# One split operation per engine over 2048 columns in place of two over 1024, in the first stage of a two-layer decoder trunk

## The chip, the cores and the metric

One core of one Trainium2 chip runs the whole kernel. The metric is the device time of one execution in microseconds (us), the median of the runs shown. One further execution was taken by the hardware profiler; durations below come from it. PE is TensorE, ACT ScalarE, DVE VectorE, POOL GpSimd, SP the SyncE queue that issues most loads.

## What is computed

Two layers act on 512 tokens of width 1024, in float32. Layer 0 is, cut to what matters here:

```python
proj = xn @ w_in          # 512x1024 @ 1024x7168: the stage of this change
a_b, a_c, a_x, a_gate, b_u, b_v, b_gate = split(proj)
y_a = a_b * conv3(a_c * a_x) * silu(a_gate)
v   = layernorm(b_v)
y_b = b_u * (tril(w_s) @ v + b_s) * silu(b_gate)
y   = concat(y_a, y_b) @ w_out
h   = h + rmsnorm(y); h = h + sigmoid(rmsnorm(h) @ w_g) * (p @ w_p)
```

Layer 1 is an mLSTM mixer with the same tail. The change touches the product `xn @ w_in` of layer 0 alone.

## The kernel before

**Split operands.** A float32 product is made of three products in the form fp32r: high by high, high by low, low by high. So each weight block in `raw7` is split: ACT copies it to `w7_hi` (line L647, in `hi7`), which rounds it, and DVE subtracts that from the block and writes `w7_lo` (L1077, in `lo7`). A block is 128 partitions by 2048 columns. Both helpers do it in two halves of 1024 columns, with one semaphore step for each half.

**Units and steps.** The 7168 output columns of layer 0 are worked in seven units (0 to 6). The product of a unit is a 2x2 block product of Strassen's kind with seven small products, p1 to p7, in place of eight. From unit 1 on their order is `ORDER = (1, 5, 6, 3, 2, 7, 4)`, here steps k0 to k6. So k2 is p6, k3 is p3, k5 is p7 and k6 is p4. On PE a small product (`product(u, p, tp)`) is two tiles tp of 12 matmuls of 512 columns (L1721, L1723, L1724). The operands of p5, p6, p7 and p4 are sums of blocks: p6's is made on DVE (`s6_add`, L1084), the others by transfers that add into `raw7`, which POOL issues (`add_in`, L525). POOL issues the one for p7 when the split of p3 is done (`late_sums`).

**Queues.** Each engine works its queue in the order written. On ACT and DVE the iteration k of unit u holds the split for the step two ahead (`hi7(7u + k + 2)`, `lo7(7u + k + 2)`). There are three buffers for split blocks (`RING = 3`), so the split for a step waits until the product three steps back has ended (`prod_done`). The split for k6 (p4) is thus in iteration k4, that for the next unit's k0 (p1) in iteration k5, that for k5 (p7) in iteration k3.

Around the splits stand the combinations of the small products. Those that matter below:

- `c_make(u, 0)` (DVE, L1155) is in iteration k2 behind `lo7`. PE's step k3 (p3) waits for it (`c_made`). In units 2 to 5 `conv` (L1202, L1205) and `c_make(u, 1)` follow it.
- `s5_make(u, 0)` (DVE; L1165, in unit 0 L1162) is in iteration k5 behind `lo7` and `z_make` (L1187) or `wide_silu` (L1209). PE's step k6 (p4) waits for it (`s5_made`).
- In units 2 to 5 iteration k4 on DVE is `lo7`, `g_make` twice, `conv`. On ACT, iterations k2 and k4 have `conv_copy` (L743, L744) ahead of `hi7`, and those copies wait for PE's `conv_transposes` (L1737, L1744) in front of steps k2 and k4.
- In unit 6 PE has `mix_transposes` (L1766) and `mix` (L1755) between steps. `mix_transposes(0)` in front of k3 waits for `mix_make(0)` (DVE, L1225), which is in DVE's iteration k2 behind `lo7` and `c_make`; `mix_transposes(1)` in front of k4 waits for `mix_make(1)`, behind `lo7` in iteration k3. On ACT, `b_copy` (L694) in iteration k1 waits for `wide_silu` of iteration k0 on DVE, behind that iteration's `lo7`; `y_high` (L759) and `s5_copy` follow.

PE's wait for the split is in `product`: half by half, on `w7_lo_ready`.

Of the kernel before, what the change touches and what calls it, by code (L numbers as in the profile page):

```python
# [25 lines left out]
F32 = mybir.dt.float32  # L26
F32R = mybir.dt.float32r
ACT = mybir.ActivationFunctionType
ALU = mybir.AluOpType
# [19 lines left out]
RING = 3  # L49
# [4 lines left out]
STEPS = [(u, p) for u in range(UNITS) for p in (ORDER if u else ORDER_FIRST)]  # L54
# [11 lines left out]
def x_buffer(u):  # L66
    return BV if u % 2 else BX


def source(u, p):  # L70

    if p in (1, 6, 4):
        return x_buffer(u)
    if p == 7 and u == 0:
        return BV
    return {5: BA, 3: BY, 7: BY, 2: BZ}[p]
# [89 lines left out]
def trunk(nc, x, p_in, slots, g_rows, ln_rows, w_mix, b_mix, conv_w, gate_bias, head_g, out):  # L166
# [3 lines left out]
    def region(at, *spec):  # L170

        made = []
        for name, shape, dtype in spec:
            size = 4
            for n in shape[1:]:
                size *= n
            made.append(nc.alloc_sbuf_tensor_at(name, shape, dtype, offset=at))
            at += (size + 31) // 32 * 32
        assert at <= nc.sbuf_usable_end, at
        return made  # L180
# [24 lines left out]
    w7_hi, w7_lo = region(W_AT, ("w7_hi", [P, RING, SLOT], F32R), ("w7_lo", [P, RING, SLOT], F32R))  # L205
    raw7, = region(R_AT, ("raw7", [P, 5, SLOT], F32))
# [125 lines left out]
    s6_sum = sem("s6_sum")  # L332
    added_in = {5: sem("s5_added_in"), 7: sem("s7_added_in"), 4: sem("s4_added_in")}
    a_in = sem("a_raw_in")
    w7_hi_ready = sem("w7_hi_ready")
    w7_lo_ready = sem("w7_lo_ready")
# [253 lines left out]
    def _(act):  # L590
# [35 lines left out]
        def hi7(g):  # L626

            u, p = STEPS[g]
            if p == 1:
                act.wait_ge(x_raw_in, 16 * (u + 1))  # L630
            if p == 2:
                act.wait_ge(z_raw_in, 16 * (u + 1))
            if p == 3:
                act.wait_ge(y_raw_in, 16 * (u + 1))
            if p == 5 and u:
                act.wait_ge(added_in[5], 16 * u)
            if p in (7, 4):
                act.wait_ge(added_in[p], 16 * (u + 1))
            if g >= RING:
                act.wait_ge(prod_done, 2 * (g - RING) + 2)  # L640
            for half in range(2):
                c = slice(half * SLOT // 2, (half + 1) * SLOT // 2)
                if p == 5 and u == 0:
                    act.wait_ge(s5_sum, half + 1)
                if p == 6:
                    act.wait_ge(s6_sum, 2 * u + half + 1)
                act.activation(w7_hi[:, g % RING, c], raw7[:, source(u, p), c], ACT.Copy).then_inc(w7_hi_ready, 1)  # L647
# [27 lines left out]
        left(0, 0, 1, 11)  # L675
        left(0, 1, 2, 12)
        hi7(0)
        x_squares(2)
        left(1, 0, 1, 11)
        left(1, 1, 2, 12)  # L680
        x_squares(3)
        left(2, 0, None, 21)
        left(2, 1, 4, None)
        hi7(1)
        left(3, 0, None, 21)
        left(3, 1, 4, None)
# [75 lines left out]
        for k in range(7):  # L762
            if k == 0:
                b_copy(0, 0)
                left_sum(5, f5)
                b_copy(0, 1)
            if k == 1:
                left_sum(6, f11)
            if k == 2:
                left_sum(3, f12)  # L770
                left_sum(7, f21)
                for tp in range(2):
                    v_copy0(a_of, 2, 0, tp, tp, a_free)
            if k == 3:
                for tp in range(2):
                    s5_copy(0, tp)
            if k == 5:
                for tp in range(2):
                    v_copy0(c_of, 3, 4, tp, tp, c_free)
            hi7(k + 2)  # L780
# [244 lines left out]
    def _(dve):  # L1025
# [44 lines left out]
        def lo7(g):  # L1070

            if g >= RING:
                dve.wait_ge(prod_done, 2 * (g - RING) + 2)
            for half in range(2):
                c = slice(half * SLOT // 2, (half + 1) * SLOT // 2)
                dve.wait_ge(w7_hi_ready, 2 * g + half + 1)
                dve.tensor_tensor(w7_lo[:, g % RING, c], raw7[:, source(*STEPS[g]), c],  # L1077
                                  w7_hi[:, g % RING, c].bitcast(F32), ALU.subtract).then_inc(w7_lo_ready, 1)
# [59 lines left out]
        left(0, 0, 1)  # L1138
        left(0, 1, 2)
        lo7(0)  # L1140
        first_norm(2)
        left(1, 0, 1)
        left(1, 1, 2)
        first_norm(3)
        left(2, 1, 4)
        less(2)
        lo7(1)
        left(3, 1, 4)
        less(3)
# [84 lines left out]
        for k in range(7):  # L1234
# [19 lines left out]
            if k == 6:  # L1254
                s5_make(0, 1)
            lo7(k + 2)
            if k == 1:
                dve.wait_ge(const_in, 16 * 6)
# [17 lines left out]
        for u in range(1, UNITS):  # L1276
            was, now = KIND[u - 1], KIND[u]
            for k in range(7):
                g = 7 * u + k
# [834 lines left out]
```

## Time and profile before

| | us |
|---|---|
| median of 3 runs | 1047.56 (1047.27 to 1047.92) |
| time of the profiled execution | 1044.74 |
| its span | 1043.0 |
| PE busy in the span | 1008.3 (97%) |
| DVE busy | 580.8 (56%) |
| ACT busy | 411.2 (39%) |

The span is from the first to the last instruction; the time has some 1.7 us more around it. A matmul row shows about 0.39 us although one starts each 0.227 us, since they overlap; so starts are what to read on PE. Steps of the changed kind run from about 59 us to 299 us of the span. In a row of the timeline "x2" means two instructions merged, and the brackets hold the idle time before it and what ended it.

### The profile page before, as it was taken

The page shows a single profiled execution, that of the slowest core. Times are in us where ns is not written, and L with a number is a line of the kernel's source. Part 1 is how long each engine was busy: PE and PEld are TensorE (multiplying, and loading weights), DVE is VectorE, ACT ScalarE, POOL GpSimd, SP SyncE. Part 2 cuts the span into 40 slices and gives each one's busy share as a digit, 9 for nine tenths or more (in the row PEclk, how much of TensorE's full clock was granted, in tenths as well). Part 3 has the DMA queues.
Part 4 walks back from the last instruction along what each step waited for, and adds up shares of the span by engine and source line. Part 5 has one row for each costly group of instructions (what it writes and reads, how often), then busy time and mean ns, then how long its engine had stood idle before and what let it go on. Part 6 is the DMA issues. An engine that isn't in the chain of part 4 may idle for free.

```text
span 1043.0 us, 12428 instructions
## 1 busy us (share of the span) xinstructions
PE 1008.3 (97%) x4586; PEld 827.1 (79%) x4586; DVE 580.8 (56%) x829; ACT 411.2 (39%) x688; POOL 74.5 (7%) x127
## 2 busy tenths in 40 slices
PE   6699999999999999999999999999999999999998
PEld 4487878878777888777888888888888888888876
DVE  5976777786874235555745433552356244541735
ACT  6544455554552234443523322332233322321622
POOL 1102100101000003102000000000000000000500
PEclk9999999999999999999999999999999999999999
DMA  8857847749361522222231232222222222153122
GB/s 323 205 175 186 204 164 198 174 149 242 54 210 41 221 82 81 98 104 81 81 121 58 80 106 80 80 80 80 80 80 80 80 81 81 41 187 117 41 81 81
DMA packets 20573, 124.90 MB, mean 120 GB/s; under 512 B 2608, under 2 KB 3632, under 8 KB 6832
## 3 DMA queue, kind: packets, MB, share of 16 engines
q1 hardware_dynamic: 17648, 103.32, 27.1%
q0 software_dynamic: 2880, 20.97, 10.4%
q8 instruction: 29, 0.48, 0.2%
q14 instruction: 16, 0.13, 0.0%
HBM read 122.18 MB, written 2.10 MB: 119 GB/s over the span
## 4 chain that ended last, share of the span: by engine, by line
PE 87%; DVE 5%; ACT 4%; issue 2%; POOL 2%; DMA 0%; POOLq 0%; DVEq 0%; ACTq 0%
PE bank L1640 11%; PE bank L1642 11%; PE bank L1641 11%; PE bank L1623 9%; PE bank L1625 9%; PE bank L1624 9%; PE bank L1721 7%; PE bank L1724 7%; PE bank L1723 7%; DVE w_lo L1077 1%; ACT square L612 1%; PE bank L1951 1%; ACT w_hi L647 1%; PE bank L1942 1%; PE bank L1954 1%
## 5 line engine op out<-in xcount | busy, mean ns | idle before, releaser
L1036 DVE TENSOR_TENSOR w_lo<-raw,w_hi 128x1024 fp32r<-128x1024 f32 x118 | 139.2, 1220 | 315.1 <-ACT w_hi L601 315.0
L601 ACT ACTIVATE w_hi<-raw 128x1024 fp32r<-128x1024 f32 x118 | 118.5, 1053 | 323.1 <-PE bank L1642 175.9
L1721 PE MATMUL bank<-w_hi,l_hi 128*128 128x512 f32 x392 | 157.1, 401 | 14.5 <-DVE bank L1155 6.9
L1623 PE MATMUL bank<-x_hi,w_hi 128*128 128x512 f32 x392 | 155.6, 397 | 0.0
L1723 PE MATMUL bank<-w_lo,l_hi 128*128 128x512 f32 x392 | 153.3, 391 | 0.0
L1724 PE MATMUL bank<-w_hi,l_lo 128*128 128x512 f32 x392 | 153.3, 391 | 0.0
L1625 PE MATMUL bank<-x_hi,w_lo 128*128 128x512 f32 x392 | 152.6, 389 | 0.0
L1624 PE MATMUL bank<-x_lo,w_hi 128*128 128x512 f32 x392 | 152.5, 389 | 0.0
L1077 DVE TENSOR_TENSOR w_lo<-raw,w_hi 128x1024 fp32r<-128x1024 f32 x98 | 115.6, 1220 | 53.8 <-ACT w_hi L647 48.6
L647 ACT ACTIVATE w_hi<-raw 128x1024 fp32r<-128x1024 f32 x98 | 98.2, 1055 | 41.0 <-DMA raw<-in_slots 21.8
L1640 PE MATMUL bank<-w_hi,x_hi 128*128 128x512 f32 x256 | 101.1, 395 | 0.1
L1721 PEld LDWEIGHTS bank<-w_hi,l_hi 128*128 128x128 f32 x392 | 74.0, 189 | 34.0 <-issue 13.9
L1642 PE MATMUL bank<-w_hi,x_lo 128*128 128x512 f32 x256 | 99.7, 390 | 0.0
L1641 PE MATMUL bank<-w_lo,x_hi 128*128 128x512 f32 x256 | 99.6, 389 | 0.0
L1640 PE MATMUL bank<-w_hi,y_hi 128*128 128x512 f32 x240 | 95.7, 399 | 0.0
L1642 PE MATMUL bank<-w_hi,y_lo 128*128 128x512 f32 x240 | 93.5, 389 | 0.0
L1641 PE MATMUL bank<-w_lo,y_hi 128*128 128x512 f32 x240 | 93.4, 389 | 0.0
L1724 PEld LDWEIGHTS bank<-w_hi,l_lo 128*128 128x128 f32 x392 | 74.0, 189 | 15.8
L1723 PEld LDWEIGHTS bank<-w_lo,l_hi 128*128 128x128 f32 x392 | 74.1, 189 | 15.7 <-issue 1.0
L1625 PEld LDWEIGHTS bank<-x_hi,w_lo 128*128 128x128 f32 x392 | 73.6, 188 | 15.5
L1624 PEld LDWEIGHTS bank<-x_lo,w_hi 128*128 128x128 f32 x392 | 73.7, 188 | 14.9
L1623 PEld LDWEIGHTS bank<-x_hi,w_hi 128*128 128x128 f32 x392 | 73.6, 188 | 14.8
(192 smaller groups left out, 1217.9 us busy)
## 6 DMA issues: line engine op xcount, KB each, us to landing
raw<-in_slots SPq DMA_DIRECT2D x87, 1024.0 KB, 4.8
raw<-in_slots POOLq DMA_DIRECT2D x20, 1024.0 KB, 8.6
h<-in_x SPq DMA_DIRECT2D x8, 512.0 KB, 6.0
out<-h SPq DMA_DIRECT2D x8, 256.0 KB, 2.0
p_sb<-in_p SPq DMA_DIRECT2D x2, 512.0 KB, 4.3
g_post<-in_g_rows SPq DMA_DIRECT2D x2, 512.0 KB, 5.9
g_ple<-in_g_rows SPq DMA_DIRECT2D x2, 512.0 KB, 6.9
g_first<-in_g_rows SPq DMA_DIRECT2D x1, 512.0 KB, 5.2
```

Source lines behind the costliest of these rows:

```text
L601: act.activation(w_hi[:, r, c], raw[:, r, c], ACT.Copy).then_inc(hi_ready, 1)
L1036: dve.tensor_tensor(w_lo[:, r, c], raw[:, r, c], w_hi[:, r, c].bitcast(F32), ALU.subtract).then_inc(lo_ready, 1)
L1077: dve.tensor_tensor(w7_lo[:, g % RING, c], raw7[:, source(*STEPS[g]), c], w7_hi[:, g % RING, c].bitcast(F32), ALU.subtract).then_inc(w7_lo ...
L1623: pe.matmul(bank[b][:, :], w[0][:, k, at], x_hi[:, k], start=(k == 0), stop=False)
L1624: pe.matmul(bank[b][:, :], w[0][:, k, at], x_lo[:, k], start=False, stop=False)
L1625: done = pe.matmul(bank[b][:, :], w[1][:, k, at], x_hi[:, k], start=False, stop=(k == KD - 1))
L1640: pe.matmul(bank[b][:, :], left_hi, w[0][:, k, c], start=(start and k == 0), stop=False)
L1641: pe.matmul(bank[b][:, :], left_hi, w[1][:, k, c], start=False, stop=False)
L1642: done = pe.matmul(bank[b][:, :], left_lo, w[0][:, k, c], start=False, stop=(stop and k == ks - 1))
L1721: pe.matmul(dst[:, :], left_hi, w7_hi[:, r, c], start=(first and k == 0), stop=False, skip_group_check=True)
L1723: pe.matmul(dst[:, :], left_hi, w7_lo[:, r, c], start=False, stop=False, skip_group_check=True)
L1724: done = pe.matmul(dst[:, :], left_lo, w7_hi[:, r, c], start=False, stop=(k == 3), skip_group_check=True)
```

## The change

In unit 0 nothing changes in the helpers; but the splits for unit 1's first two steps stand in unit 0's iterations k5 and k6, and are changed with unit 1. For steps of unit 1 and later, 42 in all, ACT makes one copy of 2048 columns and adds 2 to its semaphore, and DVE waits for the 2, makes one subtraction of 2048 columns, and adds 2 to its own. Where p6's operand is a sum made in halves, ACT waits for both halves.

```diff
@@ scalar: hi7 @@
             if g >= RING:
                 act.wait_ge(prod_done, 2 * (g - RING) + 2)
+            if u:
+                if p == 6:
+                    act.wait_ge(s6_sum, 2 * u + 2)
+                act.activation(w7_hi[:, g % RING], raw7[:, source(u, p)], ACT.Copy).then_inc(w7_hi_ready, 2)
+                return
             for half in range(2):
@@ vector: lo7 @@
             if g >= RING:
                 dve.wait_ge(prod_done, 2 * (g - RING) + 2)
+            if STEPS[g][0]:
+                dve.wait_ge(w7_hi_ready, 2 * g + 2)
+                dve.tensor_tensor(w7_lo[:, g % RING], raw7[:, source(*STEPS[g])],
+                                  w7_hi[:, g % RING].bitcast(F32), ALU.subtract).then_inc(w7_lo_ready, 2)
+                return
             for half in range(2):
```

## Rows read from the trace of the kernel before

**Rows 1.** The page's first part: busy time, share of the span, instructions.

```profile
PE 1008.3 (97%) x4586; PEld 827.1 (79%) x4586; DVE 580.8 (56%) x829; ACT 411.2 (39%) x688; POOL 74.5 (7%) x127
```

**Rows 2.** Waits from 60 to 312 us: total, times, longest.

```profile
DVE w_lo L1077 <- ACT w_hi L647: 48.1, 28, 5.1
...
PE bank L1721 <- DVE s L1165: 3.4, 5, 1.2
```

**Rows 3.** PE's timeline: start, duration, idle; the stalls ahead of k6.

```profile
102.91 0.50 PE L1721 MATMUL bank<-w_hi,l_hi 128*128 128x512 f32 x1 [1.15 <-DVE s L1165]
...
143.70 0.50 PE L1721 MATMUL bank<-w_hi,l_hi 128*128 128x512 f32 x1 [0.59 <-DVE s L1165]
...
265.91 0.50 PE L1721 MATMUL bank<-w_hi,l_hi 128*128 128x512 f32 x1 [0.45 <-DVE s L1165]
```

**Rows 4.** Groups by shape, 60 to 312 us: busy, mean ns, idle before.

```profile
L1077 DVE TENSOR_TENSOR w_lo<-raw,w_hi 128x1024 fp32r<-128x1024 f32 x84 | 99.1, 1221 | 53.3 <-ACT w_hi L647 48.1 <-PE bank L1724 4.7
L647 ACT ACTIVATE w_hi<-raw 128x1024 fp32r<-128x1024 f32 x83 | 83.3, 1054 | 40.7 <-DMA raw<-in_slots 21.8 <-PE bank L1724 18.9
...
L1231 DVE TENSOR_TENSOR y_lo<-y,y_hi 128x512 fp32r<-128x512 f32 x10 | 6.4, 682 | 0.0
L759 ACT ACTIVATE y_hi<-y 128x512 fp32r<-128x512 f32 x10 | 5.7, 621 | 0.0
```

**Rows 5.** Timeline of ACT, unit 2, iteration k4.

```profile
132.85 2.01 ACT L647 ACTIVATE w_hi<-raw 128x1024 fp32r<-128x1024 f32 x2
```

**Rows 6.** Timeline of DVE, unit 2, iterations k2, k4 and k5.

```profile
122.29 2.36 DVE L1077 TENSOR_TENSOR w_lo<-raw,w_hi 128x1024 fp32r<-128x1024 f32 x2 [2.70 <-ACT w_hi L647]
124.57 0.69 DVE L1155 TENSOR_TENSOR bank<-s,bank 128x512 f32<-128x512 f32 x1
...
134.01 2.36 DVE L1077 TENSOR_TENSOR w_lo<-raw,w_hi 128x1024 fp32r<-128x1024 f32 x2 [2.28 <-ACT w_hi L647]
...
140.03 2.35 DVE L1077 TENSOR_TENSOR w_lo<-raw,w_hi 128x1024 fp32r<-128x1024 f32 x2
...
142.97 1.27 DVE L1165 TENSOR_TENSOR s<-s,bank 128x512 f32<-128x512 f32 x2
```

**Rows 7.** PE's timeline, unit 2: k3's first matmul, the transposes before k4.

```profile
125.70 0.39 PE L1721 MATMUL bank<-w_hi,l_hi 128*128 128x512 f32 x1
...
131.15 0.60 PE L1737 MATMUL bank<-ident,z_tok 128*128 128x128 f32 x4
```

**Rows 8.** Timeline of DVE, unit 0 (k5) and unit 1 (k2, k5).

```profile
62.20 0.68 DVE L1162 TENSOR_TENSOR v_even<-s,bank 128x512 f32<-128x512 f32 x1
...
83.96 0.69 DVE L1155 TENSOR_TENSOR bank<-s,bank 128x512 f32<-128x512 f32 x1
...
97.79 2.36 DVE L1077 TENSOR_TENSOR w_lo<-raw,w_hi 128x1024 fp32r<-128x1024 f32 x2 [0.49 <-ACT w_hi L647]
```

**Rows 9.** PE's timeline: first matmul of unit 0's k6, of unit 1's k3.

```profile
63.52 0.39 PE L1721 MATMUL bank<-w_hi,l_hi 128*128 128x512 f32 x1
...
85.28 0.39 PE L1721 MATMUL bank<-w_hi,l_hi 128*128 128x512 f32 x1
```

**Rows 10.** Timeline of DVE, units 5 (k5) and 6 (k2, k3).

```profile
261.70 2.36 DVE L1077 TENSOR_TENSOR w_lo<-raw,w_hi 128x1024 fp32r<-128x1024 f32 x2 [0.81 <-ACT w_hi L647]
...
287.09 0.75 DVE L1225 SCALAR_TENSOR_TENSOR yb<-bank,b_tok,gu 128x512 f32<-128x512 f32 x1
...
294.53 0.74 DVE L1225 SCALAR_TENSOR_TENSOR yb<-bank,b_tok,gu 128x512 f32<-128x512 f32 x1
```

**Rows 11.** Timeline of ACT, unit 6, iterations k1 and k3.

```profile
277.33 0.58 ACT L694 ACTIVATE bank<-bank 128x512 f32<-128x512 f32 x1 [2.21 <-DVE th_b L1209]
...
291.09 2.01 ACT L647 ACTIVATE w_hi<-raw 128x1024 fp32r<-128x1024 f32 x2 [1.13 <-DMA raw<-in_slots]
```

**Rows 12.** PE's timeline, unit 6, the transposes ahead of k3 and k4.

```profile
288.72 0.60 PE L1766 MATMUL bank<-ident,yb 128*128 128x128 f32 x4
...
295.49 0.60 PE L1766 MATMUL bank<-ident,yb 128*128 128x128 f32 x4
```

## The prediction, made before the changed kernel ran

> **What bounds the kernel now.** I read the page's first part first. PE is busy 97% of the span, DVE 56% and ACT 39% [rows 1]. So busy time taken off DVE or ACT is worth nothing by itself. What counts is whether a result that PE waits for comes earlier or later. Second, the waits of the stage that is changed: PE hardly waits there, and never for a split. Its five waits are all for `s5_make` ahead of step k6, one in each of units 1 to 5, 3.4 us in all. In the same stretch DVE waits 28 times, 48.1 us in all, for ACT's half of the split [rows 2]. The reader is to see two things: PE's margins against DVE's queue are already used up at one place of each unit, and at more than half of the 42 splits DVE is idle until ACT's first half is there. Third, PE's timeline for the sizes of these five waits: 1.15 us in unit 1, 0.59 in each of units 2 to 4, 0.45 in unit 5 [rows 3].
>
> **One split, before and after.** Today ACT starts a split at 132.85 and DVE starts its first half at 134.01, 1.16 us later: 1.05 for the copy of 1024 columns [rows 4, 5, 6], and 0.11 until the waiting DVE starts. DVE's next instruction starts 2.28 us after that, as 122.29 to 124.57 shows [rows 6]. So from ACT's start to the end of the split, as the queue behind sees it, are 3.44 us.
>
> The trace has no operation of 2048 columns. Going from 512 to 1024 columns ACT's copy grows from 621 to 1054 ns, and DVE's subtraction from 682 to 1221 ns [rows 4]: 0.85 and 1.05 ns for a column. Twice 1024 is then, as an estimate from these four rows, 1.92 us on ACT and 2.30 us on DVE. The other bound is that merging saves nothing: 2.11 and 2.44 us, twice the single operation. I take the lower values, since the rows at 512 and 1024 columns are of the same two operations and show a part that does not grow. For DVE's queue that means 2.21 us from the start of a split to the next instruction in place of 2.28, since the second start-up goes.
>
> Now the split takes 1.92 + 0.11 + 2.21 = 4.24 us where it took 3.44. **Where DVE waits for ACT, everything behind the split in DVE's queue is 0.8 us later** (DVE starts 0.87 later and gains 0.07). Where DVE is itself late by more than 0.87 us, the change gains 0.07. With the upper bounds (0.2 more on ACT, 0.17 on DVE) the delay is 1.16 us.
>
> The Trainium skill speaks on both sides. "VectorE: DVE Perf Modes", section on the TRN2 errata, says that an operation on SBUF pays a fixed latency once, so one large tile is cheaper than several small ones. The rows agree: that is the part that does not grow. "Perfetto Trace Analysis", section "Optimizing Scalar/DVE Operations", says that where these engines are not saturated but cause bubbles on others, breaking instructions up may finish work sooner. Rows 1 to 3 describe that case, and here instructions are put together. By the first rule alone the sum would be a gain of at most 0.07 us at each place below, by the second the loss that follows.
>
> **Where the 0.8 us reach PE.** I go through the places where PE needs something that stands behind a split. From the start of `c_make` or `s5_make` to PE's first matmul are 0.73 us (142.97 to 143.70) [rows 3, 6].
>
> *Unit 0, k6.* `s5_make(0, 0)` stands behind unit 1's first split. It moves from 62.20 to 63.00, ready at 63.73; PE starts at 63.52 [rows 8, 9]. Cost 0.2.
>
> *Unit 1, k3.* `c_make(1, 0)` moves from 83.96 to 84.76, ready at 85.49; PE starts at 85.28 [rows 8, 9]. Cost 0.2; its chain starts from PE, so it keeps its distance to a shifted PE.
>
> *Unit 1, k6.* DVE waits 0.49 us for ACT at 97.79 [rows 8], so the split is exposed, and PE already waits. Cost 0.8, or 0.85, since the late splits of k3 and k4 also leave DVE free only just in time.
>
> *Units 2 to 5, k3.* DVE waits 2.70 us for ACT ahead of 122.29, so this split is exposed: DVE starts it at 123.16, and `c_make` moves from 124.57 to 125.37, ready at 126.10. PE starts k3 at 125.70 [rows 6, 7]. Cost 0.4 in each unit. From unit 2's k6 to unit 5's are (265.91 - 143.70) / 3 = 40.74 us for a unit [rows 3]; units 3 to 5 repeat unit 2's rows here.
>
> *Units 2 to 4, k6.* From 134.01 to 142.97 DVE's queue has no gap: split of p4, `g_make`, `conv`, split of p1, `z_make`, `s5_make` [rows 6]. Its head waits for ACT, whose start 132.85 follows PE's transposes at 131.15 [rows 5, 7]. The head's delay of 0.8 goes through whole, less 0.07 at the second split, which was not waiting for ACT by enough to count. PE waits there already. Cost 0.73 in each.
>
> *Unit 5, k6.* DVE waits 0.81 us for ACT at 261.70 [rows 10]. Cost 0.8.
>
> *Unit 6, ahead of k3.* Two exposed splits stand in one chain: that of iteration k0 delays `wide_silu`, for which `b_copy` waits [rows 11], and ACT works on without a gap to the split of iteration k2, whose DVE half precedes `mix_make(0)`. Its two splits delay it by 1.5, ACT's merged copy giving back 0.1. It ends at 287.84 today, and PE's transposes start at 288.72 [rows 10, 12], a margin of 0.85. Cost 0.65.
>
> *Unit 6, ahead of k4.* The adding transfer for p7 is issued when p3's split is done, 1.6 late. ACT waits for that transfer at 291.09 [rows 11], so p7's split starts 1.6 late and ends 2.4 late, and `mix_make(1)` behind it as well. It ends at 295.27 today for a start at 295.49 [rows 10, 12]: margin 0.2. Of 2.4, 0.2 are margin and 0.65 the shift that PE has by then. Cost 1.55. Behind k4 the chain starts anew from PE, and I find margins of more than 0.8.
>
> In units 1 to 5 the transfer for p7 is late as well, but DVE is idle 2.28 us ahead of 134.01 [rows 6], which takes it up. SP's loads stand behind `w7_lo_ready` too and move by 0.8 to 1.6; none is next to a margin that I could find. PE's own waits by halves cost nothing: its splits are done more than a microsecond ahead, and a full block late by 0.8 still is in time.
>
> Sum: 0.2 + 0.2 + 0.85 + 4 x 0.4 + 3 x 0.73 + 0.8 + 0.65 + 1.55 = 8.0 us; the second tile of k3 in units 2 to 5 adds 0.05 in each (`c_make(u, 1)` ends 0.8 late too), so 8.2. After the stage PE goes on without idle time, so nothing absorbs it. The profiled time would go from 1044.74 to 1052.9. I put the difference on the median of the runs, 2.8 us above that execution: 1047.56 + 8.2 = 1055.8 us.
>
> **Rivals.**
>
> *Only k6 pays.* The waits at k3 and in unit 6 rest on margins of 0.2 to 0.85 us, read to a tenth or two. If they hold (a release a little faster, a transfer that lands sooner when issued later), there remain the places where PE waits today: 0.85 + 3 x 0.73 + 0.8 = 3.8 us, 1051.4 us. Against it: four margins of the same kind would have to be wrong.
>
> *Merging saves nothing.* With 1.16 us for each exposed split: the sum above is 14 delays of 0.8 less some 3 us of margins; 14 x 1.16 - 3 = 13.2, so 1060.8 us. The rows of 512 columns speak against it.
>
> *Hidden anyway (not slower).* PE never waits for `w_lo`, so if something other than the split led to `s5_make` (say, `z_make`'s wait for ACT's copy, or PE's own product), a later split would be free: 1047.6 us. For it: PE waits only 3.4 us in the stage. Against it: the DVE queue has no gap from 134.01 to `s5_make`. It decides only if that queue could take 0.8 us, and it has no room.
>
> *The fixed part wins (faster).* If ACT were ahead of DVE by a whole copy at the splits on the chain, each would gain 0.07, twice a unit in five units: 0.7 us, 1046.9 us, and at the very most the 3.4 us that PE waits now. Rows 2 show the opposite order. This is what the errata section of the Trainium skill's "VectorE: DVE Perf Modes" would promise.
>
> **Chances.** My forecast 0.62; only k6 pays 0.16; merging saves nothing, or the delays stack up further in unit 6, 0.12; hidden 0.07; faster 0.03. The predicted time is that of the first, its own range 1053.5 to 1058 (a tenth of a microsecond on each of 14 delays, and unit 6's transfer). The range for 8 in 10 reaches down to the second case and part of the way to the third: 1051.2 to 1060.0 us. A difference of 0.2%, 2.1 us, is about what a measurement of this kernel can tell from none. Slower by more: 0.62 + 0.16 + 0.12 = 0.90. Within: 0.07. Faster: 0.03.
>
> **What the changed profile would show.** L647 and L1077 each with 42 operations of 2048 columns at about 1.92 and 2.30 us. DVE's wait for ACT up from 48.1 us by some 0.87 for each of 28. PE's waits ahead of k6 about 2.0 us in unit 1, 1.3 in units 2 to 5. New waits of PE for `c_make` (L1155) ahead of k3, 0.2 to 0.45 us; in unit 6 new waits of the transposes L1766 for `yb`, 0.65 and 1.5 us. The period from unit 2's k6 to unit 5's up from 40.74 to about 41.9 us. The time behind unit 6 unchanged. I would be wrong if the operations of 2048 columns cost something else than the sum of their columns, if ACT started its copies earlier than today, or if a transfer that collides with others now lands at another time.

## The result, and the profile after

The changed kernel took 1056.76 us (median of 4 runs, 1056.31 to 1057.34), the one before beside it 1047.41 us (4 runs, 1045.17 to 1047.92): ratio 1.0098, 95% interval 1.0082 to 1.0115 (the record's estimate; the two medians alone give 1.0089). By the medians it is 9.35 us slower; 8.2 was forecast, in a range that holds the result. The profiled execution took 1056.79 us with a span of 1055.1 us.

The page of the changed kernel, its busy engines and the two groups of the merged operations:

```profile
PE 1014.4 (96%) x4586; PEld 829.1 (79%) x4586; DVE 578.3 (55%) x787; ACT 407.3 (39%) x646; POOL 75.0 (7%) x127
...
L1081 DVE TENSOR_TENSOR w_lo<-raw,w_hi 128x2048 fp32r<-128x2048 f32 x42 | 96.2, 2290 | 69.1 <-ACT w_hi L644 58.0
...
L644 ACT ACTIVATE w_hi<-raw 128x2048 fp32r<-128x2048 f32 x42 | 80.4, 1914 | 45.0 <-DMA raw<-in_slots 25.0
```

They answer to [rows 1] and [rows 4]. In them the first number behind the bar is the busy time in us, the second the mean ns of one. Both engines do less: 2.5 us less busy on DVE, 3.9 on ACT, 42 instructions fewer on each. The merged operations take 2.290 and 1.914 us; 2.30 and 1.92 were estimated. The change does what it says, and the kernel is slower.

The same view of waits as [rows 2], of the changed kernel from 60 to 325 us:

```profile
DVE w_lo L1081 <- ACT w_hi L644: 58.0, 33, 7.0
...
PE bank L1731 <- DVE s L1175: 7.3, 5, 2.0
...
PE bank L1776 <- DVE yb L1235: 2.0, 2, 1.4
PE bank L1731 <- DVE bank L1165: 1.0, 4, 0.3
```

PE waited 3.4 us in this stage [rows 2] and now waits 10.3. The three kinds are those that the prediction named: `s5_make` ahead of k6, `mix_make` in unit 6, `c_make` ahead of k3. PE's timeline shows the places (unit 1 k6, unit 2 k3 and k6, unit 5 k6, unit 6 ahead of k3 and of k4):

```profile
105.57 0.50 PE L1731 MATMUL bank<-w_hi,l_hi 128*128 128x512 f32 x1 [1.97 <-DVE s L1175]
...
128.78 0.50 PE L1731 MATMUL bank<-w_hi,l_hi 128*128 128x512 f32 x1 [0.26 <-DVE bank L1165]
129.12 0.40 PE L1733 MATMUL bank<-w_lo,l_hi 128*128 128x512 f32 x1
...
147.72 0.50 PE L1731 MATMUL bank<-w_hi,l_hi 128*128 128x512 f32 x1 [1.34 <-DVE s L1175]
...
274.06 0.50 PE L1731 MATMUL bank<-w_hi,l_hi 128*128 128x512 f32 x1 [1.27 <-DVE s L1175]
...
297.61 0.66 PE L1776 MATMUL bank<-ident,yb 128*128 128x128 f32 x4 [0.59 <-DVE yb L1235]
...
305.98 0.66 PE L1776 MATMUL bank<-ident,yb 128*128 128x128 f32 x4 [1.40 <-DVE yb L1235]
```

How the overlap went, in unit 2 on ACT and DVE:

```profile
136.12 1.92 ACT L644 ACTIVATE w_hi<-raw 128x2048 fp32r<-128x2048 f32 x1
```

```profile
138.17 2.29 DVE L1081 TENSOR_TENSOR w_lo<-raw,w_hi 128x2048 fp32r<-128x2048 f32 x1 [2.34 <-ACT w_hi L644]
140.38 0.41 DVE L1203 SCALAR_TENSOR_TENSOR th_a<-th_a,bank 128x256 f32<-128x256 f32 x1
...
144.12 2.28 DVE L1081 TENSOR_TENSOR w_lo<-raw,w_hi 128x2048 fp32r<-128x2048 f32 x1
...
146.99 1.27 DVE L1175 TENSOR_TENSOR s<-s,bank 128x512 f32<-128x512 f32 x2
```

ACT starts at 136.12, DVE at 138.17: 2.05 us where it was 1.16 [rows 5, 6]. The next instruction starts at 140.38, so the split takes 4.26 us in place of 3.44. From there to `s5_make` at 146.99 nothing on DVE is idle, as before, and PE starts at 147.72, 0.73 us later.

**From 9.4 to 12.1 us.** The two profiled spans differ by 12.1 us, more than the medians. The difference between equal points of PE's timeline ([rows 3, 12] and above) is 2.66 us at unit 1's k6, 4.02 at unit 2's, 8.15 at unit 5's and 10.49 at unit 6's transposes ahead of k4; it is then constant to 1004.17 (993.70 before). Two parts of it are stretches in which the granted clock of TensorE differs. Windows of both kernels, before the first merged split is used and near the end (the columns are busy times by engine, then the clock):

```profile
52.00:60.00 8.00, 8.00 (x27) 6.38 (x26) 2.85 (x4) 1.24 (x3) 0.00 (x0) 0.71 0.68 264
...
1000.00:1010.00 10.00, 8.13 (x38) 6.44 (x37) 8.83 (x11) 6.28 (x12) 2.02 (x2) 0.83 0.34 118
```

```profile
52.00:60.00 8.00, 8.00 (x32) 6.43 (x31) 2.85 (x5) 2.32 (x4) 0.00 (x0) 0.85 0.66 260
...
990.00:1000.00 10.00, 8.13 (x43) 6.50 (x41) 8.37 (x11) 5.82 (x11) 1.56 (x2) 1.00 0.39 135
```

The first fence is the changed kernel, the second the one before. In the first pair the changed kernel stays at the lower of the two levels (1.2 GHz, a matmul each 0.43 us in place of 0.227) until 56.6 us, the one before until 54.4: 1.1 us. In the second pair it falls to it for some microseconds, and the one before does not, though both have the same work: 1.6 us. 12.1 - 1.1 - 1.6 = 9.4 us is what the change costs at an equal clock. The first part can't come from the change, since ACT starts its first merged copy only at 59.85. For the second this isn't shown. All nine timed executions of the changed kernel, here and in changed_again below, have a mean clock of 0.992 or 0.993; of the 17 of the kernel before beside changed_again, seven have 0.993 or less and ten have 0.994 to 0.996. That the medians here say 9.35 as well is in part chance: beside changed_again they are 10.9 us apart.

### The profile page after: what moved, and what is told of

Its sections match the earlier page's. It is cut to its first block, busy times and chain, and to the rows that moved or that the text cites. A ratio compares the mean times of both kernels' runs of the same rounds, so it can differ in the third digit from the quotient of the medians.

```text
span 1055.1 us, 12344 instructions
## 1 busy us (share of the span) xinstructions
PE 1014.4 (96%) x4586; PEld 829.1 (79%) x4586; DVE 578.3 (55%) x787; ACT 407.3 (39%) x646; POOL 75.0 (7%) x127
## 3 DMA queue, kind: packets, MB, share of 16 engines
q0 software_dynamic: 2880, 20.97, 10.3%
## 4 chain that ended last, share of the span: by engine, by line
PE 80%; DVE 7%; ACT 5%; issue 4%; POOL 2%; DMA 1%; POOLq 0%; DVEq 0%; SPq 0%; ACTq 0%
PE bank L1650 11%; PE bank L1652 10%; PE bank L1651 10%; PE bank L1633 8%; PE bank L1635 8%; PE bank L1634 8%; PE bank L1731 6%; PE bank L1734 5%; PE bank L1733 5%; ACT w_hi L644 2%; DVE w_lo L1081 1%; ACT square L612 1%; PE bank L1961 1%; PE bank L1952 1%; PE bank L1964 1%
## 5 line engine op out<-in xcount | busy, mean ns | idle before, releaser
L1041 DVE TENSOR_TENSOR w_lo<-raw,w_hi 128x1024 fp32r<-128x1024 f32 x118 | 139.2, 1221 | 315.1 <-ACT w_hi L601 315.0
L601 ACT ACTIVATE w_hi<-raw 128x1024 fp32r<-128x1024 f32 x118 | 118.5, 1054 | 324.4 <-PE bank L1652 178.0
L1081 DVE TENSOR_TENSOR w_lo<-raw,w_hi 128x2048 fp32r<-128x2048 f32 x42 | 96.2, 2290 | 69.1 <-ACT w_hi L644 58.0
L644 ACT ACTIVATE w_hi<-raw 128x2048 fp32r<-128x2048 f32 x42 | 80.4, 1914 | 45.0 <-DMA raw<-in_slots 25.0
```

What stands on the lines that cost most here:

```text
L601: act.activation(w_hi[:, r, c], raw[:, r, c], ACT.Copy).then_inc(hi_ready, 1)
L1041: dve.tensor_tensor(w_lo[:, r, c], raw[:, r, c], w_hi[:, r, c].bitcast(F32), ALU.subtract).then_inc(lo_ready, 1)
L1081: dve.tensor_tensor(w7_lo[:, g % RING], raw7[:, source(*STEPS[g])], w7_hi[:, g % RING].bitcast(F32), ALU.subtract).then_inc(w7_lo_ready, 2)
```

## The experiments

The kernels of a group ran on one chip beside the kernel before (15 to 23 runs of it). Ratios are to it; they are the record's estimates and differ by up to 0.13% from the quotients of the medians. Its single executions lie between 1044.7 and 1050.0 us, so a difference under 0.15% says little, and I read PE's waits in the stage beside each ratio. "PE waits" is the total in the view of waits from 60 to 325 us; before: 3.4 us. "Stage" is how much longer PE takes over the stage by its timeline, from the same matmul in unit 0 (58.98 us in the kernel before, 60.07 in the changed one) to the same transposes behind the stage (337.70 and 348.21). In the profiles of wait_both, act_merged and merged_to_unit_5 the clock falls for some microseconds near 107 us; about 1.5 us is taken off there, an estimate from matmuls that start each 0.43 us in place of 0.227.

| kernel | ratio (95% interval) | PE waits, us | stage, us |
|---|---|---|---|
| changed_again | 1.0105 (1.0087 to 1.0122) | 10.2 | 9.5 |
| wait_both | 1.0133 (1.0117 to 1.0148) | 12.4 | 11.5 |
| dve_merged | 1.0125 (1.011 to 1.014) | 11.8 | 10.9 |
| act_merged | 1.012 (1.0104 to 1.0135) | 11.1 | 10.3 |
| merged_on_path | 1.0115 (1.01 to 1.013) | 9.8 | 9.0 |
| merged_off_path | 1.0015 (1.0005 to 1.0025) | 4.0 | 1.0 |
| merged_to_unit_5 | 1.0072 (1.0055 to 1.0089) | 8.3 | 7.3 |
| quarters | 0.9993 (0.9984 to 1.0002) | 2.4 | -1.0 |
| s5_early | 0.9969 (0.996 to 0.9978) | 1.5 | -3.1 |
| s5_early_merged | 1.0047 (1.0034 to 1.006) | 5.3 | 3.2 |
| s5_early_to_5 | 0.996 (0.9947 to 0.9974) | 0.4 | -4.2 |
| s5_early_to_5_quarters | 0.9963 (0.995 to 0.9976) | 0.3 | -4.2 |

### The overlap alone, with nothing merged: wait_both

The theory: the time is lost because DVE can't start on the first half while ACT makes the second. The rival: the large operations cost it themselves.

```diff
             for half in range(2):
                 c = slice(half * SLOT // 2, (half + 1) * SLOT // 2)
-                dve.wait_ge(w7_hi_ready, 2 * g + half + 1)
+                dve.wait_ge(w7_hi_ready, 2 * g + (2 if STEPS[g][0] else half + 1))
```

> Nothing is merged: both engines keep two operations of 1024 columns, only DVE's first subtraction of a split (unit 1 and later) waits for ACT's second copy as well. If the loss comes from the lost overlap of the two engines, this kernel shows it without any large operation: DVE starts 2.01 + 0.11 = 2.12 us after ACT's start in place of 1.16, 0.96 us later, and gains nothing, against 0.86 - 0.07 = 0.79 in the changed kernel. Over 14 delays in a chain less some 3 us of margins that is 2.4 us more than the changed kernel, so about 11.5 us over the kernel before (ratio 1.011; 1.008 to 1.014). If the large operations themselves cost the time (their length, their double semaphore step), this kernel is equal to the one before, 1.000.

Measured 1.0133, 14 us, against 11.5 forecast, within its stated bounds and above the changed kernel; by PE's timeline the stage costs 11.5 us. Unit 2 on PE, ahead of k3 and k6:

```profile
130.06 0.50 PE L1721 MATMUL bank<-w_hi,l_hi 128*128 128x512 f32 x1 [0.39 <-DVE bank L1155]
...
149.23 0.50 PE L1721 MATMUL bank<-w_hi,l_hi 128*128 128x512 f32 x1 [1.54 <-DVE s L1165]
```

These are the waits of the changed kernel, 0.13 and 0.2 us longer. No operation is larger than before. So the lost overlap is enough for the whole loss, and merging gives a small part back.

### One engine merged: act_merged and dve_merged

act_merged is the changed kernel without its edit of `lo7`:

```diff
-            if STEPS[g][0]:
-                dve.wait_ge(w7_hi_ready, 2 * g + 2)
-                dve.tensor_tensor(w7_lo[:, g % RING], raw7[:, source(*STEPS[g])],
-                                  w7_hi[:, g % RING].bitcast(F32), ALU.subtract).then_inc(w7_lo_ready, 2)
-                return
```

> ACT makes one copy of 2048 columns, DVE keeps two subtractions of 1024. Lost overlap: DVE starts as late as in the changed kernel and lacks its 0.07 us of gain, so 14 x 0.07 = 1 us more than that kernel: about 10.3 us over the one before (ratio 1.010). If DVE's large subtraction were the cost, it would be near 1.000.

dve_merged is the changed kernel without its edit of `hi7`:

```diff
-            if u:
-                if p == 6:
-                    act.wait_ge(s6_sum, 2 * u + 2)
-                act.activation(w7_hi[:, g % RING], raw7[:, source(u, p)], ACT.Copy).then_inc(w7_hi_ready, 2)
-                return
```

> ACT keeps two copies of 1024 columns, DVE makes one subtraction of 2048 behind both. DVE starts 2.12 us after ACT's start, as in wait_both, but gains 0.07 by its single operation: 0.89 late in place of 0.96. Over the chain of some 14 delays that is 1 us less than wait_both, so 13 us over the kernel before (ratio 1.0125), and above the changed kernel. If merging on DVE alone were the gain of the change, it would be below the changed kernel.

Both are slower than the kernel before by about as much as forecast, and the order is the forecast one in PE's waits: 10.2 us with both merged, 11.1 with ACT alone, 11.8 with DVE alone, 12.4 with neither but the wait. The ratios lie in the same order, though their intervals overlap. The stage costs 9.4, 10.3, 10.9 and 11.5 us in that order; 10.3 was forecast for ACT alone and 11.5 for the wait alone. The wait ahead of unit 2's k6 in the two, act_merged first:

```profile
149.18 0.50 PE L1726 MATMUL bank<-w_hi,l_hi 128*128 128x512 f32 x1 [1.48 <-DVE s L1170]
```

```profile
147.87 0.50 PE L1726 MATMUL bank<-w_hi,l_hi 128*128 128x512 f32 x1 [1.44 <-DVE s L1170]
```

### Which splits: merged_on_path, merged_off_path, merged_to_unit_5

```diff
+ON_PATH = [g for g in range(7, 49) if (g - 2) % 7 in (2, 4, 5) or g >= 44]
+MERGED = lambda g: g in ON_PATH             # merged_on_path
+MERGED = lambda g: g >= 7 and g not in ON_PATH   # merged_off_path
+MERGED = lambda g: 7 <= g < 43              # merged_to_unit_5
...
-            if u:
+            if MERGED(g):
...
-            if STEPS[g][0]:
+            if MERGED(g):
```

> Merged only where the prediction found a way to PE: the splits of iterations k2, k4 and k5, and all from unit 6's k0 on (22 of 42 steps). By the prediction's places the whole loss is here: 9 us over the kernel before, within 0.7 us of the changed kernel (ratio 1.009). If the loss is spread over all merged splits by count, it is 22/42 of it, 4.9 us (1.0047).

> The other 20 steps merged: the splits of iterations k0, k1, k3 and k6 of units 1 to 5 (and of unit 0's k6). By the prediction's places none is near PE: equal to the kernel before (ratio 0.9995 to 1.001). By count it would be 20/42 of the loss, 4.5 us (1.0043).

The expectations say 22 and 20 steps; the condition selects 21, and the other 21 are left. The 21 on the path cost 9.0 of the 9.4 us. The other 21 cost 0.15% and not the half of the loss that is their share by number. But they are not free, as I had said. PE's timeline of merged_off_path has one wait that the kernel before has not, the second of these:

```profile
144.23 0.50 PE L1733 MATMUL bank<-w_hi,l_hi 128*128 128x512 f32 x1 [0.62 <-DVE s L1177]
...
296.97 0.44 PE L1778 MATMUL bank<-ident,yb 128*128 128x128 f32 x2 [0.47 <-DVE yb L1237]
```

It stands in unit 6 ahead of k4, where the margin was 0.2 us [rows 10, 12]. The only merged split near it is that of unit 5's iteration k6. From it leads a chain that I had overlooked: split of p5, `s6_add`, `gu_make` on DVE, `wide_tanh` and the split of p6 on ACT, `b_copy`, the split of p3, the adding transfer for p7, `mix_make(1)`. In the changed kernel this chain has 0.8 us more room, because PE itself is held up by 0.8 us ahead of unit 5's k6. That room doesn't hold all of it. From unit 5's iteration k4 on, merged_on_path differs from the changed kernel by this one split alone. Its `mix_make(0)` is earlier and PE's wait ahead of k3 shorter. The first fence is the changed kernel, the second merged_on_path, each with rows of ACT, DVE and PE:

```profile
280.21 1.20 ACT L739 ACTIVATE th_b<-bank 128x512 f32<-128x512 f32 x2 [5.38 <-DVE gu L1224]
...
296.81 0.74 DVE L1235 SCALAR_TENSOR_TENSOR yb<-bank,b_tok,gu 128x512 f32<-128x512 f32 x1
...
297.61 0.66 PE L1776 MATMUL bank<-ident,yb 128*128 128x128 f32 x4 [0.59 <-DVE yb L1235]
```

```profile
279.75 1.19 ACT L741 ACTIVATE th_b<-bank 128x512 f32<-128x512 f32 x2 [4.95 <-PE bank L1736]
...
296.34 0.75 DVE L1237 SCALAR_TENSOR_TENSOR yb<-bank,b_tok,gu 128x512 f32<-128x512 f32 x1
...
297.14 0.65 PE L1778 MATMUL bank<-ident,yb 128*128 128x128 f32 x4 [0.21 <-DVE yb L1237]
```

With the split merged `wide_tanh` (the rows of ACT) waits for `gu_make`, without it for PE. So 0.38 of the changed kernel's 0.59 us come from a split that the prediction had off the path. In merged_off_path the stage costs 1.0 us, two thirds of it at the wait ahead of k4; the rest of the 0.15% I can't tell from the spread.

> Merged in all steps whose split stands ahead of unit 5's iteration k6 (36 of 42); unit 5's k6 and unit 6 in halves. By the places of the prediction PE keeps the waits at k3 and k6 of units 1 to 5 and loses the two in unit 6, measured at 0.59 and 1.40 us with 0.3 of slower first operations: 2.2 us less than the changed kernel, 7.2 over the one before (ratio 1.007). By count of merged splits it would be 36/42 of the loss, 8.1 us.

Measured 1.0072, and 2.0 us below the changed kernel that ran beside it (1054.85 against 1056.83 us). The waits ahead of k6 stay as in the changed kernel, 1.37 us in unit 2, and the two of unit 6 are gone:

```profile
148.64 0.50 PE L1732 MATMUL bank<-w_hi,l_hi 128*128 128x512 f32 x1 [1.37 <-DVE s L1176]
```

The stage costs 7.3 us for 7.2 forecast. So unit 6's part of the loss has the forecast size.

> The changed kernel itself, beside the others on one chip, as their common reference: 9.4 us over the kernel before (ratio 1.009 to 1.011).

It gave 1.0105, inside the forecast interval, 10.9 us by the medians for 9.4 forecast. The stage costs 9.5 us; the rest fits the clock part named above.

### The other way: quarters

```diff
+            if u:
+                for q in range(4):
+                    c = slice(q * SLOT // 4, (q + 1) * SLOT // 4)
+                    if p == 6:
+                        act.wait_ge(s6_sum, 2 * u + q // 2 + 1)
+                    act.activation(w7_hi[:, g % RING, c], raw7[:, source(u, p), c], ACT.Copy).then_inc(w7_hi_ready, 1)
+                return
...
+                for q in range(4):
+                    c = slice(q * SLOT // 4, (q + 1) * SLOT // 4)
+                    dve.wait_ge(w7_hi_ready, 4 * g - 14 + q + 1)
+                    done = dve.tensor_tensor(w7_lo[:, g % RING, c], raw7[:, source(*STEPS[g]), c],
+                                             w7_hi[:, g % RING, c].bitcast(F32), ALU.subtract)
+                    if q % 2:
+                        done.then_inc(w7_lo_ready, 1)
```

> Four copies and four subtractions of 512 columns. ACT 0.62 us for the first, so DVE starts 0.73 us after ACT in place of 1.16; four subtractions take 4 x 0.60 = 2.40 in place of 2.28. So the split ends at 3.13 us in place of 3.44 where DVE waits for ACT, 0.3 us earlier. PE waits only in five places today: in units 2 to 4 p4's split is 0.3 earlier and p1's 0.12 longer, so 0.2 us each, 0.3 in units 1 and 5. About 1.2 us faster than before (ratio 0.999; 0.9975 to 1.000). If small operations cost more than they overlap, it is slower, 1.001 to 1.003.

```profile
143.73 0.50 PE L1737 MATMUL bank<-w_hi,l_hi 128*128 128x512 f32 x1 [0.44 <-DVE s L1181]
```

PE's waits fall from 3.4 to 2.4 us, as forecast (0.59 to 0.44 in unit 2). The time's interval holds both the forecast 0.999 and no change: the direction is right in the trace (the stage gains 1.0 us of the 1.2 forecast), and inconclusive in the time.

### Taking the queue behind the split away: s5_early, s5_early_merged

In iteration k5 `z_make` or `wide_silu` and `s5_make(u, 0)` go ahead of the split on DVE, in units 1 to 6:

```diff
+                if k == 5:
+                    for tp in range(2):
+                        if now == "a":
+                            z_make(u, a_of, tp, tp, a_free)
+                        else:
+                            wide_silu(u, a_of, tp, tp, a_free)
+                    s5_make(u, 0)
                 if g + 2 < 7 * UNITS:
                     lo7(g + 2)
```

(the same lines go from their place behind the split).

> Halves as before; in iteration k5 of units 1 to 6 z_make or wide_silu and s5_make(u, 0) stand ahead of the split on DVE's queue. s5_make(u, 0) then waits only for PE's tile 0 of step k5 and is ready some 2 us before PE wants it; p1's split, due 5 us later, takes the delay. The five waits ahead of k6 (3.4 us) and the slower first matmul behind each (0.1 us) go: 3.9 us faster than before (ratio 0.9963). If the waits are by something else, no change.

> The changed kernel with the same order. The waits ahead of k6 go here too; what is left of the loss are k3 of units 1 to 5 (0.25 to 0.4 us each with the first matmul, 1.9 in all), unit 6 (2.3) and unit 0's k6 (0.3), less the 3.9 us of waits that the kernel before has: 0.5 us over the kernel before (ratio 1.0005; 0.9985 to 1.003). If the merged operations cost PE time in another way, the loss stays near 9 - 3.9 = 5 us (1.005).

The first held: all five waits ahead of k6 are gone, 0.9969. Two new ones came in unit 6, ahead of k4 and of k6 (the expectation of s5_early_to_5 places the first ahead of k3, which is wrong), so the stage gains 3.1 us and not 3.9:

```profile
291.83 0.33 PE L1766 MATMUL bank<-ident,yb 128*128 128x128 f32 x1 [0.47 <-DVE yb L1225]
...
306.60 0.66 PE L1766 MATMUL bank<-ident,yb 128*128 128x128 f32 x4 [1.00 <-DVE yb L1225]
```

The second failed: 1.0005 was forecast and 1.0047 measured, outside its bounds; the stage costs 3.2 us for 0.5 forecast. PE's timeline of it, unit 2 ahead of k3 and unit 6 ahead of k3, k4 and k6:

```profile
126.39 0.50 PE L1731 MATMUL bank<-w_hi,l_hi 128*128 128x512 f32 x1 [0.26 <-DVE bank L1165]
...
290.37 0.66 PE L1776 MATMUL bank<-ident,yb 128*128 128x128 f32 x4 [2.16 <-DVE yb L1235]
...
298.55 0.66 PE L1776 MATMUL bank<-ident,yb 128*128 128x128 f32 x4 [1.19 <-DVE yb L1235]
...
313.27 0.66 PE L1776 MATMUL bank<-ident,yb 128*128 128x128 f32 x4 [1.00 <-DVE yb L1235]
```

The waits ahead of k6 are gone here too, and those ahead of k3 unchanged. But in unit 6 PE waits 4.3 us where the changed kernel waits 2.0. I take it for the chain of merged_off_path: in the changed kernel PE's own wait ahead of unit 5's k6 (1.27 us) gave it room, and with that wait gone the delays of p5's, p6's and p3's splits come through. s5_early speaks for it: without a merged split, and with PE's wait of 0.45 us ahead of unit 5's k6 [rows 3] gone, it has a wait of 0.47 us ahead of k4 where the kernel before has none. The wait of 1.00 us is in s5_early as well: there the moved `s5_make(6, 0)` holds up `mix_make(3)`.

### A kernel that beats both: s5_early_to_5

```diff
-                if k == 5:
+                if k == 5 and u < UNITS - 1:       # ahead of the split
...
+                if k == 5 and u == UNITS - 1:      # behind it, as before
```

> As s5_early, but unit 6 keeps its order. In s5_early PE waits 1.00 us in unit 6 ahead of k6 for mix_make(3), which the moved s5_make holds up. That wait goes with its slow first operation; the one of 0.47 us ahead of k3 stays. 1.0 us faster than s5_early, 4.3 us faster than before (ratio 0.9958).

> The same with splits in quarters, which end 0.3 us earlier where DVE waits for ACT. PE's one remaining wait of the stage is 0.47 us, behind a chain of at least two such splits: it goes. 0.5 us faster than s5_early_to_5 (ratio 0.9953 to the kernel before). If the longer DVE queue (0.12 us for a split) counts instead, it is equal or slower.

s5_early_to_5 measured 0.996 (1042.64 against 1045.89 us), and the wait of 1.00 us is gone. One is left:

```profile
292.19 0.55 PE L1773 MATMUL bank<-ident,yb 128*128 128x128 f32 x3 [0.43 <-DVE yb L1225]
```

It stands ahead of k4. In quarters that one goes too (the 0.3 us in the table stand ahead of unit 0's k6, with "issue" as what ended them, which means nothing that the profile shows), but the time is the same within the interval (0.9963). Against s5_early the forecast 1.0 us can't be told from the times either (0.996 and 0.9969, with overlapping intervals); the stage shows 1.1 us. Sure is that both beat the kernel before.

## Why the prediction was right

Place by place, forecast against the shift of PE between equal points of the two timelines, the early clock part of 1.1 us taken off:

| place | forecast, us | measured, us |
|---|---|---|
| unit 0, k6 | 0.2 | 0.3 |
| unit 1, k3 and k6 | 1.05 | 1.3 |
| units 2, 3 and 4, k3 and k6 | 1.18 each | 1.36, 1.38, 1.32 |
| unit 5, k3 and k6 | 1.25 | 1.43 |
| unit 6, ahead of k3 and k4 | 2.2 | 2.34 |
| sum | 8.2 | 9.4 |

**The bound.** Right: PE's margins against DVE's queue set the price, and less work on DVE and ACT was worth nothing. wait_both shows that the overlap is the cause, since it has the loss without the merged operations.

**The cost of one split.** 0.8 us forecast, 4.26 - 3.44 = 0.82 in unit 2. Both operations came within 0.01 us of the estimate from the groups of 512 and 1024 columns, so the bound in which merging saves nothing is out.

**The places.** PE is late at all named places and at no other in the changed kernel (at unit 0's k6 and unit 1's k3 only by the shift of 0.3 us in each, the view lists no wait there); merged_on_path has 9.0 of the 9.4 us. The statement that the rest has no way to PE was wrong: the split of unit 5's k6 has one. Unit 6 ahead of k3 is therefore right in number partly by luck. The prediction reached 0.65 us with two splits in the chain; with those two alone PE shifts by 0.36 us there (merged_on_path: 297.14 - 288.72 = 8.42, after 8.06 at unit 5's k6), and by 0.74 with the third.

**The size.** 1.2 us too small, spread over all places. The term that was mis-sized is mainly the price of a new wait. I counted the time from release to PE's first matmul and no more. But the first matmul after a wait is followed by the next after 0.34 us (128.78 to 129.12) and not 0.227. The waits ahead of k6 had this before the change as well; for the new ones ahead of k3 it adds 0.11 us each. In unit 2, the first starts 0.42 us late (128.78 against 125.70 + 2.66), as forecast, and k6's wait is 0.75 us longer, as forecast; with the 0.11 that is 1.28 of 1.36. The remaining 0.08 are 0.02 in the next matmuls and 0.06 in the second tile of k3, for which the forecast had 0.05 (shift 3.19 at 129.12, 3.21 at 131.41, 3.27 at 133.51). Over all new waits this term is about 0.8 of the 1.2 us, an estimate from these shifts (0.13 us at k3 of units 2 to 5, about 0.1 at units 0 and 1, 0.06 for the transposes in unit 6). The last 0.4 are spread over k6 and unit 6, and I can't place them for certain.

**What I expected to see and did not.** DVE's wait for ACT was to grow by 0.87 us for each of 28 waits. It grew from 48.1 to 58.0 us over 33. DVE itself arrives later at many of them, behind the split before, so a delay is not added at each. Also, the view puts part of these waits down to PE (11.1 us, 4.7 before in [rows 4]), although DVE's wait for ACT ends after it, since ACT waits for the same product; all idle time ahead of the split grew from 53.3 to 69.1 us. The period from unit 2's k6 to unit 5's rose from 40.74 to (274.06 - 147.72) / 3 = 42.1 us, for 41.9 forecast.

**The rivals.** "Only k6 pays" is out by the waits at k3 and in unit 6. "Hidden anyway" and "the fixed part wins" are out by the result. The section "Optimizing Scalar/DVE Operations" of the Trainium skill's "Perfetto Trace Analysis" named the right side of the trade: with DVE at 56% and ACT at 39%, cutting finer helps where PE waits (quarters: its waits down by 1.0 us). The saving of the errata section in the Trainium skill's "VectorE: DVE Perf Modes" is there too, 0.07 us for a split on DVE's queue, less than a tenth of the 0.87 us that the lost overlap costs.

## What to carry to other kernels

Two operations in a chain of two engines are not only two fixed costs: the second engine works on the first half while the first makes the second. Before merging, read how long the second engine waits for the first, and follow what stands behind the operation in its queue to the next thing that the bounding engine waits for. And a margin is measured against the bounding engine as it runs now: if one of its waits is removed, chains that this wait covered can come out further on, as unit 6 of s5_early and s5_early_merged suggests. Here the better edit was to order the queue, so that what PE waits for stands ahead of a split that PE needs only after the next 24 matmuls.

## What the runs showed of the hardware

- Single executions of the kernel before lie up to 5 us apart (1044.7 to 1050.0), and the granted clock of TensorE accounts for part of it. In the two profiles 1.1 us come from 2.2 us more at the lower level early on, and 1.6 us from a fall near 1003 us (0.83 in that window against 1.00), with the same instructions in both.
- In three of the seven profiles in which PE waits some 2 us ahead of unit 1's k6 the clock falls about 1 us behind that wait, and in four it does not. wait_both waits 2.10 us until 105.11, and then, in a window of the same columns as above:

```profile
102.00:112.00 10.00, 7.90 (x28) 6.03 (x27) 8.56 (x12) 2.69 (x4) 0.00 (x0) 0.83 0.03 8
```

- The matmul behind a waiting one starts 0.34 us after it, 0.11 more than in a running sequence. Behind a row of transposes the first product matmul is followed nearly as late without a wait: 131.94 to 132.26, 0.32 us, in the kernel before.
- ACT's copy grew from 1.054 to 1.914 us and DVE's subtraction from 1.221 to 2.290 us for twice the columns: 0.84 and 1.04 ns for a column, and 0.19 and 0.15 us that do not grow.
